# A one-column Silu ahead of the expert loop in a decoder step with a hierarchical mixture of experts

## The reference

```python
def expert_block(args):
    xblk, e = args
    h = jax.nn.silu(xblk @ w_gate[e]) * (xblk @ w_up[e])
    return h @ w_down[e]

yb = lax.map(expert_block, (xb, blk_exp))
y = yb[dest] * sg[:, None]
return jax.ops.segment_sum(y, st, num_segments=n_tok)
```

## Time and profile before

| | us |
|---|---|
| three executions | 2995.17, 2995.5, 3009.73 |
| median | 2995.5 |
| the profiled execution, its time | 3000.02 |
| its span in the trace | 2998.3 |
| mean granted clock of TensorE | 0.958 |

### The profile page before, as it was taken

How to read it: one execution, slowest core, us unless ns; L and a number is a source line. 1 busy time by engine, 2 the same in 40 slices (tenths; PEclk the granted TensorE clock), 3 DMA queues, 4 the chain that set the end, 5 groups by cost and what they waited for, 6 DMA issues and landing times. The chain is left out here.

```text
span 2998.3 us, 46714 instructions
## 1 busy us (share of the span) xinstructions
PE 2689.6 (90%) x16568; PEld 1711.1 (57%) x16570; DVE 1964.6 (66%) x3027; ACT 1513.8 (50%) x2553; POOL 766.2 (26%) x1012
## 2 busy tenths in 40 slices
PE   8999999999898988979887888999996889898977
PEld 6887888799897444545455654654554333333322
DVE  2599523689943798787786647544446566666648
ACT  2111222369794687786878657310100565656636
POOL 3334432233322033341334331104110100000015
PEclk9999999999998999999999999999997899999989
DMA  4222232123443212201100348347334577867548
GB/s 138 97 91 93 98 112 84 43 81 115 133 134 118 79 49 62 73 8 49 33 12 12 107 176 270 130 155 243 126 121 158 202 261 264 313 257 266 192 175 322
DMA packets 237910, 408.68 MB, mean 136 GB/s; under 512 B 29148, under 2 KB 153308, under 8 KB 229034
## 3 DMA queue, kind: packets, MB, share of 16 engines
q1 hardware_dynamic: 174322, 242.93, 24.4%
q0 software_dynamic: 24464, 86.40, 8.0%
q10 hardware_dynamic: 38960, 77.18, 7.0%
HBM read 313.11 MB, written 93.24 MB: 136 GB/s over the span
## 5 line engine op out<-in xcount | busy, mean ns | idle before, releaser
L471 PE MATMUL p_ps_acc<-p_x_hi,p_w_hi 128*128 128x352 f32 (+2 forms) x1480 | 528.7, 357 | 13.0 <-POOL p_w_lo L398 11.2
L471 PE MATMUL p_ps_acc<-p_x_lo,p_w_hi 128*128 128x352 f32 (+2 forms) x1480 | 519.7, 351 | 0.0
L471 PE MATMUL p_ps_acc<-p_x_hi,p_w_lo 128*128 128x352 f32 (+2 forms) x1480 | 519.4, 351 | 0.0
L471 PEld LDWEIGHTS p_ps_acc<-p_x_hi,p_w_hi 128*128 128x128 f32 (+1 forms) x1480 | 276.9, 187 | 66.7 <-issue 18.8
L471 PEld LDWEIGHTS p_ps_acc<-p_x_lo,p_w_hi 128*128 128x128 f32 (+1 forms) x1480 | 277.2, 187 | 27.6 <-issue 0.5
L471 PEld LDWEIGHTS p_ps_acc<-p_x_hi,p_w_lo 128*128 128x128 f32 (+1 forms) x1480 | 276.8, 187 | 27.0
L3208 PE MATMUL e_ps_G<-l_wgu,e_xT 128*32 x656 | 289.8, 595 | 1.0 <-ACT e_xT L3265 1.0
L3208 PE MATMUL e_ps_G<-g_late,e_xT 128*32 128x512 f32 x1312 | 290.2, 594 | 0.0
L3208 PE MATMUL e_ps_G<-g_shared,e_xT 128*32 128x512 f32 x656 | 289.7, 595 | 0.0
L626 ACT ACTIVATE p_stage<-p_ps_acc,g_cols 128x352 f32<-128x352 f32 (+3 forms) x145 | 88.5, 610 | 334.3 <-PE p_ps_acc L471 334.2
L396 POOL CAST p_w_hi<-g_late 128x1024 fp32r<-128x1024 f32 x74 | 93.4, 1263 | 590.5 <-PE p_ps_acc L471 433.8
(11 more groups left out here) (597 smaller groups left out, 5841.0 us busy)
## 6 DMA issues: line engine op xcount, KB each, us to landing
g_late<-in_w_in_dram SPq DMA_DIRECT2D x72, 512.0 KB, 3.8
l_wgu<-in_w_gate_dram SPq DMA_DIRECT2D x32, 1024.0 KB, 6.0
l_wgu<-in_w_up_dram SPq DMA_DIRECT2D x32, 1024.0 KB, 8.8
l_wd<-in_w_down_dram SPq DMA_DIRECT2D x28, 1024.0 KB, 5.6
yb<-e_y ACTq DMA_DIRECT2D x41, 512.0 KB, 3.5
featT<-p_stage ACTq DMA_DIRECT2D x28, 528.0 KB
featT<-p_stage ACTq DMA_DIRECT2D x28, 512.0 KB
g_late<-featT SPq DMA_DIRECT2D x56, 256.0 KB, 5.1
```

The source lines that it names most:

```text
L471: m = nc.tensor.matmul(acc[slot][tb][0:rows, 0:width], wp[:, slot, k, 0:rows], xp[:, k, at], start=(k == 0 and i == 0), stop=(k == KD - 1 ...
```

## The change

One instruction is written ahead of ACT's part of `experts`: Silu over one column of the identity matrix, into the first column of `sg`. Nothing reads that value: the first `silu` of the loop overwrites all of `sg`.

```diff
--- before.py
+++ after.py
@@ -3308,6 +3308,7 @@
                         copy_down(e)
                     store(b, j)
 
+                nc.scalar.activation(sg[:, 0:1], c.ident[:, 0:1], ACT.Silu)
                 e = last_of(0)
                 keep_x(0)
                 copy_gate_up(e)
```

## The result

The changed kernel took 2969.5 us, the median of four executions (2960.4 to 2973.9), against 2998.5 us for the kernel before, now also of four (2995.2 to 3009.7). The ratio is 0.9893 with a 95% interval of 0.9856 to 0.9930. 2958 was forecast, a ratio of 0.9875, with a range of 2950 to 2973. The profiled execution took 2967.4 us, its span went from 2998.3 to 2965.7 us, 32.6 us less.

The account below looks back on a forecast made before the run. TensorE was taken as the bound, losing time between `up` and `turn_hidden`. Loads of 25.7 us plus clock falls of 11.6 us gave 37.3 us off the median of 2995.5, forecast 2958 us, range 2950 to 2973.

Parts of the forecast that it names:

- PE is the bound, and waits at one place for the chain over ACT and DVE: In the `experts` loop TensorE sets the pace, losing 47.0 us in 41 waits between `up` and `turn_hidden`.
- 20 x 1.283 = 25.7 us for the loads: ACT's 20 table loads ahead of `silu` in even groups leave the loop, a gain of 25.7 us.
- 11.6 us for the falls of the clock: Eight falls of TensorE's clock behind even groups' `silu` vanish, 1.45 us each; bounds 0 and 11.6 us.
- 0 of 20 against 8 of 20: Falls of the granted clock behind `silu`: none in 20 odd groups, eight in 20 even ones; basis for the 11.6 us.
- The added pair costs 0: One load and one one-column activation at the phase's start are covered by ACT's idle time; uncovered 1.7 us, once.
- The weights are not late: Shorter groups in the loop ask for weights sooner, but SP has lead; cost taken as 0, bound 5.9 us.
- What follows moves forward as a whole: Behind the loop, `combine` waits for the last store of `yb`, so it starts earlier; loop's end 37 us earlier.
- The load stays in the loop: The no-change case: table loads remain in the loop's body and the time stays as before; chance 0.03.
- A switch costs 2.66 us: Rival: each table switch in the loop also hides a drain, so 65 us go, time 2931; chance 0.02.
- The clock keeps falling: Rival: loads leave the loop but as many falls stay; gain 25.7 us, time 2969.8; chance 0.12.
- late weights: Rival: PE in the loop waits for weight landings, up to 5.9 us, time 2958 to 2964; chance 0.03.
- The clock falls in all groups: Slower rival: short even idle times at `turn_hidden` bring falls in all 41 groups, 22 us longer, time 3018; chance 0.03.

Follow-up runs that it names:

- the copy experiments: Changed kernel plus an unread ACT copy ahead of even `silu` (ratio 0.9997), of all `silu` (3049.1 us), or half the copy ahead of all (3007.5 us).
- the whole copy ahead of all `silu`: Changed kernel plus an unread ACT copy of 1408 columns ahead of all 41 `silu`; one execution, 3049.1 us, loop 570.52 us.
- the second trace of the changed kernel: The changed kernel itself, unaltered, run again with more rounds; ratio 0.9871 to the kernel before, loop 508.21 us.
- the second comparison: The changed kernel again (four executions) against the kernel before (thirteen), both slower; ratio 0.9871 (0.9853 to 0.9888).
- Exp ahead: Changed kernel with the added one-column activation as Exp instead of Silu; ratio 1.0009 to the kernel before, loop 544.02 us.
- the 80 loads: Changed kernel plus a one-column Exp and Silu behind the store in each of 40 groups, where ACT is idle; ratio 0.9871, median 2981.7 us.

## Why the prediction was right, step by step

- **PE is the bound, and waits at one place for the chain over ACT and DVE.** Right. 25.7 us of these waits went and the loop became shorter by at least as much.
- **20 x 1.283 = 25.7 us for the loads.** Right. The waits fell from 47.0 to 21.3 us, which is 25.7; the 21.7 of the prediction does not follow from its own 47.0 - 25.7 (0.52 us in each of 40 groups and 0.9 in the 41st would give it). That odd groups show what even ones would become held to 0.01 us.
- **11.6 us for the falls of the clock.** Right in size and sign: 37.2 us in the loop against 37.3. The argument "0 of 20 against 8 of 20" turned out to be good, though the prediction had no cause for it; the copy experiments supply the part of the cause that lies in the wait. The reading of the stretches was off in one point: they begin 0.06 us behind the end of PE's wait, not where it is nearly over, and the fall at 2428.4 begins some 0.6 us behind it. And the frequency did not carry over: 8 of 20 made me expect 16 falls with the whole copy ahead of all `silu`, and there were 7. What saved this term is that after the change no group has the long wait, so no frequency was needed.
- **The added pair costs 0.** Right, with more room than I had worked out (4.84 us of idle time left instead of 2.3). The activation took 203 ns, not the 391 ns of the nearest row.
- **The weights are not late.** Right. SP's waits for PE went from 157.4 to 133.8 us in 15 cases, so the lead shrank but held:

```profile
SPq L2933 <- PE e_ps_G L3208: 133.8, 15, 26.0
```

- **What follows moves forward as a whole.** Right within the scatter of the traces. In the first trace 2.3 us were lost ahead of the first `silu`, so that the last one came 34.9 us earlier and not 37, and 2.3 us behind it. These 4.6 us are the difference between the 37.2 us of the loop and the 32.6 us of the span; the second trace of the changed kernel does not show them.
- **The time.** 2958 was forecast and 2969.5 measured, inside the range. Of the 11.5 us, 3.0 are the base: I set the gain against a median of three, 2995.5, and the fourth execution moved that to 2998.5. The rest is the gain itself, 29.0 us between the two medians where 37.3 was forecast, and 40.3 us in the second comparison. Medians of four executions with a spread of 13 to 15 us in either kernel are too coarse to judge the sum; the loop, with 37.2 us in the trace, judges it. The ratios, 0.9893 and 0.9871, have intervals that both hold the forecast's 0.9875.
- **The rivals.** "The load stays in the loop" is what happens with Exp ahead, and the compiled order had told the two apart before any run. "A switch costs 2.66 us" falls by the rows of the 80 loads. "The clock keeps falling" and "late weights" did not occur. "The clock falls in all groups" did not occur either: there was no fall at 0.51 or 1.13 us, and even with 1.8 us in all groups it fell in 7 of 40.

## What to carry to other kernels

In the kernels here an ACT_TABLE_LOAD stood in the loop's body when the table on the way into the loop differed from the one at its end; a one-column activation of the loop's own function ahead of it moved the load out. Look first whether the loads are on the path: compare the turns of the loop that have one with those that have none. And a cost that only lengthens a wait of TensorE can be dearer than it looks, if the wait grows long enough for the clock to fall (here 26 us of delay cost 37). With the same 47 us of waits, the loop with 20 long and 20 short ones had eight falls and the one with even ones in between had none; so look at the longest single wait as well as at the sum.

## What the runs showed of the hardware

- A table load of ACT takes 1.283 us also directly behind other work of ACT, with 0.01 us on either side (80 loads in idle time). It costs the loop nothing where ACT would have been idle, and its full length between PE's `up` and `silu`.
- TensorE's clock fell to 1.2 GHz behind single waits of 1.8 us (8 of 20 groups; 7 of 40 with the same wait in all), and in these loops never behind waits of 0.51 or 1.13 us. A fall lasts some 3.4 us in both patterns (2428.4 to 2431.7, 2398.6 to 2402.0) and costs 1.45 us in the one and 1.70 us in the other.
- A wait on PE that stands ahead of another wait and a semaphore increment costs 0.15 us more, where it is the late one, than the same wait placed last (12.71 against 12.56 us for a group, one trace each).
